# Relative-bias tables of a two-block decoder on Trainium2: skewed DMA reads in place of reversing matmuls, and another place for the small products

## What is computed

```python
def swiglu(x, w_gate, w_up, w_down):
    return (jax.nn.silu(x @ w_gate) * (x @ w_up)) @ w_down

def head_bias(table, dist):
    return jnp.moveaxis(table[rel_bucket(dist)].astype(jnp.float32), -1, 0)

# diff_attention, one block of 128 queries
dist = qpos[:, None] - kpos[None, :]
s = jnp.einsum('bqhcd,bkhcd->bchqk', qi, k, preferred_element_type=jnp.float32) * scale
s = s + head_bias(bias_table, dist)[None, None]
```

## Time and profile before

| | |
|---|---|
| median of 3 runs | 3522.79 us (3521.4 to 3523.41) |
| profiled execution, its own time | 3524.35 us |
| its span in the trace | 3522.6 us |
| PE busy | 3349.7 us, 95% |
| DVE / ACT / POOL busy | 1847.8 / 1566.2 / 143.4 us |
| mean DMA rate | 164 GB/s |
| chain that ended last | PE 88%, DVE 6%, ACT 4% |

### The profile page before, as it was taken

The page is one execution under the profiler, slowest core; times in us unless marked ns, Lnnn a source line. Parts: engine busy times, 40 slices in busy tenths (PEclk is TensorE's granted clock), DMA queues, the critical chain, the costliest instruction groups (busy, mean ns, idle before and its releaser), DMA issues.

```text
span 3522.6 us, 39807 instructions
## 1 busy us (share of the span) xinstructions
PE 3349.7 (95%) x16471; PEld 2785.5 (79%) x16471; DVE 1847.8 (52%) x2387; ACT 1566.2 (44%) x1918; POOL 143.4 (4%) x253
## 2 busy tenths in 40 slices
PE   8999999949999999999999999989999999999998
PEld 6898888737888888878888788977788788867886
DVE  5456454565455555455464554643554645534645
ACT  4344444424444444344344344455543544555444
POOL 0000000012000000000000000022000000121000
PEclk9999999969999999999899999989999999999999
DMA  6545555413555545555455545642455556523553
GB/s 209 191 156 179 191 180 191 157 60 112 190 180 191 168 144 191 179 184 187 143 178 183 177 156 190 169 126 96 135 192 173 173 187 179 144 97 119 188 188 111
DMA packets 323904, 576.24 MB, mean 164 GB/s; under 512 B 45257, under 2 KB 130352, under 8 KB 323596
## 3 DMA queue, kind: packets, MB, share of 16 engines
q1 hardware_dynamic: 321196, 566.71, 49.6%
q0 software_dynamic: 2384, 6.63, 0.7%
q10 hardware_dynamic: 144, 0.35, 0.0%
HBM read 571.53 MB, written 1.08 MB: 163 GB/s over the span
## 4 chain that ended last, share of the span: by engine, by line
PE 88%; DVE 6%; ACT 4%; issue 1%; DMA 0%; DVEq 0%; SPq 0%; ACTq 0%
PE up L1663 20%; PE up L1664 19%; PE up L1665 19%; PE acc L1663 8%; PE acc L1665 8%; PE acc L1664 8%; DVE w_lo L939 2%; ACT w_hi L559 2%; PE up L1938 1%; PE acc L1833 1%; PE up L2154 1%; DVE xT_lo L1051 1%; PE acc L1760 1%; ACT xT_hi L624 0%; PE acc L1840 0%
## 5 line engine op out<-in xcount | busy, mean ns | idle before, releaser
L939 DVE TENSOR_TENSOR w_lo<-raw,w_hi 128x2048 fp32r<-128x2048 f32 x543 | 1244.3, 2292 | 1349.2 <-ACT w_hi L559 1346.5
L559 ACT ACTIVATE w_hi<-raw 128x2048 fp32r<-128x2048 f32 x543 | 1040.7, 1917 | 1467.5 <-PE up L1665 1091.0
L1663 PE MATMUL up<-w_hi,xT_hi 128*128 128x512 f32 (+1 forms) x2500 | 993.5, 397 | 66.3 <-DVE xT_lo L1051 26.8
L1664 PE MATMUL up<-w_lo,xT_hi 128*128 128x512 f32 (+1 forms) x2500 | 982.5, 393 | 0.0
L1665 PE MATMUL up<-w_hi,xT_lo 128*128 128x512 f32 (+1 forms) x2500 | 981.8, 393 | 0.0
L1663 PEld LDWEIGHTS up<-w_hi,xT_hi 128*128 128x128 f32 x2500 | 476.1, 190 | 179.5 <-issue 47.0
L1665 PEld LDWEIGHTS up<-w_hi,xT_lo 128*128 128x128 f32 x2500 | 476.1, 190 | 99.4
L1664 PEld LDWEIGHTS up<-w_lo,xT_hi 128*128 128x128 f32 x2500 | 476.5, 191 | 94.6
L1663 PE MATMUL acc<-w_hi,ff_hi 128*128 128x512 f32 x1216 | 480.3, 395 | 3.5 <-DVE ff_lo L1070 3.5
L1665 PE MATMUL acc<-w_hi,ff_lo 128*128 128x512 f32 x1216 | 474.0, 390 | 0.0
L1664 PE MATMUL acc<-w_lo,ff_hi 128*128 128x512 f32 x1216 | 473.4, 389 | 0.0
(11 more groups left out here) (282 smaller groups left out, 2360.2 us busy)
## 6 DMA issues: line engine op xcount, KB each, us to landing
raw<-in_ffn_down SPq DMA_DIRECT2D x88, 1024.0 KB, 4.8
raw<-in_ffn_gate SPq DMA_DIRECT2D x80, 1024.0 KB, 5.1
raw<-in_ffn_up SPq DMA_DIRECT2D x80, 1024.0 KB, 5.1
raw<-in_ffn_wi SPq DMA_DIRECT2D x80, 1024.0 KB, 5.2
raw<-in_ffn_wo SPq DMA_DIRECT2D x44, 1024.0 KB, 4.8
raw<-in_w_in SPq DMA_DIRECT2D x38, 1024.0 KB, 5.1
raw<-in_conv_w_in SPq DMA_DIRECT2D x24, 1024.0 KB, 5.2
raw<-in_w_branch SPq DMA_DIRECT2D x12, 1024.0 KB, 5.0
```

The source lines that it names most:

```text
L559: nc.scalar.activation(w_hi[n % RING][:], raw[n % RING][:], ACT.Copy).then_inc(hi_ready, 1)
L939: nc.vector.tensor_tensor(w_lo[n % RING][:], raw[n % RING][:], w_hi[n % RING][:].bitcast(F32), ALU.subtract).then_inc(lo_ready, 1)
L1663: pe.matmul(ps, lh, rh, start=start, stop=False)
L1664: pe.matmul(ps, lh, rl, start=False, stop=False)
```

## The change

The tables stages move behind norms 8, 9 and 11, each directly in front of a feed-forward, and `after` and the two tests of `turned_x` look past them. The small products of part 1 are written into the banks up[2] and up[3], ahead of `first_pair`, which uses up[0] and up[1]; the feed-forward then waits for DVE's copies (`tab_dve`) before its second pair of banks. DVE scales the rows while it copies them. POOL stores every row 128 times, 383 elements each (20 x 128 rows) and a longer row of 511 for eight heads (8 x 128), and reads them with a skew of 382 (510) elements per partition straight into T and TCW. DVE picks TC out of TCW in part 2, which waits for both reads. The 30 products of 128x8, U, and the 10 reversing products with their copies are gone. The convolution's work area moves to another place in the arena.

```diff
--- before.py
+++ after.py
@@ -101,11 +101,9 @@
         plan += [("conv", i // 3)] if i % 3 == 0 else [("mla",)] if i == 1 else [("sg",)]
         plan += [("norm", 3 * i + 2), ("ffn", 1, i, 1)]
 
-    at = plan.index(("norm", 9))
-    plan[at:at] = [("tables", 0)]
-    at = plan.index(("norm", 10))
-    plan[at:at] = [("tables", 1)]
-    plan += [("tables", 2)]
+    for part, row in enumerate((8, 9, 11)):
+        at = plan.index(("norm", row)) + 1
+        plan[at:at] = [("tables", part)]
     for i in range(2):
         plan += [("norm", 12 + 4 * i), ("ffn", 2, i, 0), ("norm", 13 + 4 * i), ("mix", i)]
         plan += [("norm", 14 + 4 * i), ("ffn", 2, i, 1), ("norm", 15 + 4 * i), ("ple", i)]
@@ -188,8 +186,8 @@
 
         T = carve(0, 20, 256)
         TC = carve(5120, 8, 2 * NCMP)
-        U = carve(5376, 20, 256)
-        rv = carve(10496, 2, 384)
+        TCW = carve(5376, 8, 384)
+        rv_a, rv_c = arena[0:12, 10496:11008], arena[0:8, 13204:13588]
         lp = carve(11264, 2, 4, 64)
         prows = arena[0:64, 11776:11904]
         relb = arena[0:33, 11904:11924]
@@ -323,7 +321,8 @@
         fin_in = sem("fin_in")
         w2_in = sem("w2_in")
         fin_ready = sem("fin_ready")
-        scratch = nc.dram_tensor("bias_rows", (20, 384), F32, kind="Internal").ap()
+        scratch = nc.dram_tensor("bias_rows", (20, P, 383), F32, kind="Internal").ap()
+        scratch_cmp = nc.dram_tensor("cmp_rows", (8, P, 511), F32, kind="Internal").ap()
         vn_ready = sem("vn_ready")
         stored = sem("stored")
 
@@ -496,7 +495,7 @@
 
         def after(i):
 
-            return next((s for s in plan[i + 1:] if s[0] != "norm"), ("end",))
+            return next((s for s in plan[i + 1:] if s[0] not in ("norm", "tables")), ("end",))
 
         block = ctx.enter_context(nc.Block())
 
@@ -775,12 +774,9 @@
                 owed.append(n0 + 11)
 
             def tables(part):
-                arrive()
-                arrive()
-                settle()
                 if part != 1:
                     return
-                act.wait_ge(tab_dve, seen.next(tab_dve))
+                act.wait_ge(tab_dve, seen.next(tab_dve, 2))
                 nc.scalar.activation(ssh[:, 4:8], ssh[:, 0:4], ACT.Exp).then_inc(tab_act, 1)
 
             def mix(s, n0):
@@ -1366,15 +1362,27 @@
 
             def tables(part):
 
-                residual()
-                settle()
                 if part == 0:
+                    nc.vector.memset(rv_a[:, 384:512], NEG / HSCALE)
                     nc.vector.memset(relb, NEG).then_inc(arena_free, 1)
                     return
                 if part == 2:
-                    flipped_tables()
+                    dve.wait_ge(u_in, seen.next(u_in, 32))
+                    for t in range(NT):
+                        at = 159 - P * t
+                        last = nc.vector.tensor_copy(TC[:, :, NCMP * t:NCMP * t + NCMP],
+                                                     TCW[:, :, at:at + 16 * (NCMP - 1) + 1:16])
+                    dve.wait_ge(tab_act, seen.next(tab_act))
+                    for i in range(2):
+                        step(nc.vector.tensor_tensor(neglam[:, i:i + 1], ssh[:, 5 + 2 * i:6 + 2 * i],
+                                                     ssh[:, 4 + 2 * i:5 + 2 * i], ALU.subtract))
+                        step(nc.vector.tensor_scalar(neglam[:, i:i + 1], neglam[:, i:i + 1], -LAM_INIT[i], None, ALU.add))
                     return
                 dve.wait_ge(tables_in, seen.next(tables_in, 16 * 8))
+                dve.wait_ge(tab_pe, seen.next(tab_pe))
+                nc.vector.tensor_scalar(rv_a[:, 0:384], up[2][0:12, 0:384], 1.0 / HSCALE, None, ALU.mult)
+                nc.vector.tensor_scalar(rv_c, up[3][0:8, 0:384], 1.0 / HSCALE, None, ALU.mult).then_inc(rv_ready, 1)
+                nc.vector.tensor_copy(pos2[:].rearrange("p i v j -> p (i v j)"), up[2][:, 384:448]).then_inc(tab_dve, 1)
                 for i in range(2):
                     for j in range(2):
                         last = nc.vector.tensor_tensor_reduce(nwt[:], lp[:, i, 2 * j, :], lp[:, i, 2 * j + 1, :], 1.0, 0.0,
...
-                dve.wait_ge(tab_dve, seen.next(tab_dve))
-
-                dve.wait_ge(tab_pe, seen.next(tab_pe))
-                nc.vector.tensor_copy(rv[0:12, 0, :], acc[0][0:12, 0:384])
-                nc.vector.tensor_copy(rv[0:8, 1, :], acc[1][0:8, 0:384]).then_inc(rv_ready, 1)
...
-            def flipped_tables():
-                for g in range(10):
...
@@ -1945,6 +1930,8 @@
                 drain_banks()
                 gates, ups_ = [up[0][:], up[1][:]], [up[2][:], up[3][:]]
                 first_pair(n, FW, gates)
+                if held:
+                    pe.wait_ge(tab_dve, seen.next(tab_dve))
                 n += 2
                 for c in range(NFC):
                     if c > 1:
@@ -1982,38 +1969,14 @@
                 residuals[0] -= 1
 
             def tables(part):
-                if part == 0:
+                if part != 1:
                     return
-                if part == 2:
-                    flipped_tables()
-                    return
+                drain_banks()
                 pe.wait_ge(tables_in, seen.next(tables_in, 16 * 8))
-                pe.wait_ge(tab_dve, seen.next(tab_dve))
-                pe.matmul(acc[0][0:12, 0:384], relb[:, 0:12], one_hots[:, 0:384], start=True, stop=True)
-                pe.matmul(acc[1][0:8, 0:384], relb[:, 12:20], one_hots[:, 384:768], start=True,
-                          stop=True)
-                pe.transpose(acc[2][:, 0:64], prows, ident[0:64, 0:64])
-                for t in range(NT):
-                    for b in range(NCMP):
-
-                        at = C_OHF - C_KEPT + 256 + P * t - 16 * b - 31
-                        i = NCMP * t + b
-                        last = pe.matmul(acc[3][:, 8 * i:8 * i + 8], one_hots[:, at:at + P], relb[:, 4:12], start=True,
-                                         stop=True)
-                last.then_inc(tab_pe, 1)
-                pe.wait_ge(tab_dve, seen.next(tab_dve))
-
-            def flipped_tables():
-
-                pe.wait_ge(u_in, seen.next(u_in, 16))
-                pe.wait_ge(x_ready, QUARTERS * (1 + residuals[0]))
-                for g in range(10):
-                    if g >= 4:
-                        pe.wait_ge(tab_dve, seen.next(tab_dve))
-                    pe.matmul(acc[g % 4][:], consts[:, C_FLIP:C_FLIP + P],
-                              U[:, 2 * g:2 * g + 2, :].rearrange("p h j -> p (h j)"), start=True,
-                              stop=True).then_inc(tab_pe, 1)
-                pe.wait_ge(tab_dve, seen.next(tab_dve, 4))
+                pe.wait_ge(arena_free, 1)
+                pe.matmul(up[2][0:12, 0:384], relb[:, 0:12], one_hots[:, 0:384], start=True, stop=True)
+                pe.matmul(up[3][0:8, 0:384], relb[:, 12:20], one_hots[:, 384:768], start=True, stop=True)
+                pe.transpose(up[2][:, 384:448], prows, ident[0:64, 0:64]).then_inc(tab_pe, 1)
 
             def mix(s, n0):
 
@@ -2298,7 +2261,7 @@
                     mix(s, n0)
                 elif s[0] == "ple":
                     ple(s, n0)
-                if s[0] not in ("norm", "final"):
+                if s[0] not in ("norm", "tables", "final"):
                     turned_x = s[0] == "mix"
                 residuals[0] += s[0] not in ("norm", "tables", "final")
 
@@ -2362,12 +2325,19 @@
                                        A["nsa_cmp_pos_2"][i, v].rearrange("(j q) d -> j (q d)", q=2)
                                        ).then_inc(tables_in, 16)
                 pool.wait_ge(rv_ready, 1)
-                pool.dma_start(scratch[0:12, :], rv[0:12, 0, :]).then_inc(rv_stored, 16)
-                pool.dma_start(scratch[12:20, :], rv[0:8, 1, :]).then_inc(rv_stored, 16)
-                pool.wait_ge(rv_stored, 32)
-
-                askew = bass.AP(scratch.tensor, 0, [[1, P], [384, 20], [1, 256]])
-                pool.dma_start(U, askew).then_inc(u_in, 16)
+                def copies(row, n):
+
+                    return row.rearrange("h (o n) -> h o n", o=1).broadcast_to([n, P, row.shape[1]])
+
+                pool.dma_start(scratch[0:12], copies(rv_a[:, 0:383], 12)).then_inc(rv_stored, 16)
+                pool.dma_start(scratch[12:20], copies(rv_c[:, 0:383], 8)).then_inc(rv_stored, 16)
+                pool.dma_start(scratch_cmp, copies(rv_a[4:12, 0:511], 8)).then_inc(rv_stored, 16)
+                pool.wait_ge(rv_stored, 48)
+
+                askew = bass.AP(scratch.tensor, P - 1, [[382, P], [383 * P, 20], [1, 256]])
+                pool.dma_start(T, askew).then_inc(u_in, 16)
+                askew_cmp = bass.AP(scratch_cmp.tensor, P - 1, [[510, P], [511 * P, 8], [1, 384]])
+                pool.dma_start(TCW, askew_cmp).then_inc(u_in, 16)
 
             def mix(s):
 

...
```

More of the change, by code:

```diff
@@ L163, in build @@
         g_rows = arena[0:G_ROWS, 0:D]
-        zconv = carve(0, 2, TOK + 2)
-        yconv = carve(520, 2, TOK)
```

(6 more changed lines are left out.)

14 lines of the change are left out of this document (removed).

## The result

The changed kernel takes **3555.4 us** (median of 4 runs, 3553.86 to 3558.12) against 3522.1 us of the kernel before beside it (4 runs, 3521.03 to 3523.41). The ratio is 1.0096, 95% interval 1.0081 to 1.0111: slower by 33 us, where 46 us less was forecast. The profiled run took 3554.6 us, its span is 3552.8 us.

What follows compares the result with a forecast made beforehand. PE was taken to bound the kernel (busy 95%, 88% of the chain), so only shortening its queue counted. Removed 48.2 us less added 2.0 gave -46.2 from 3522.79, so 3476.6 us; range 3474 to 3494.

Steps and rivals of the forecast that it cites:

- Removed work, norms 9, 10 and 12: Boundaries at these norms, priced against sisters without a tables stage: gains of 7.7, 22.5 and 18.0 us, together 48.2 us.
- the further 1.7 us from the clock: Norm 10: a possible extra gain of 1.7 us on the diagonal products if the clock holds.
- Small work in front of the feed-forward: Behind norm 9: small products and PE's waits for `tab_dve` and the fourth tile add 2.0 us, bounds 1.2 and 5.
- Rival 1: Feed-forward behind norm 9: small work makes the fifth tile slip too, one period of 5.4 us lost, 3481; chance 0.06.
- Part 2 and the reads: Behind norm 11: small copies cost nothing (1 us without cover); reads fit, 58 us of transfers in about 290 us.
- rival 3: Part 2: skewed reads not back, DVE and all low parts wait; about 3725 us with a single engine; chance 0.04.
- The transfers: Behind norm 9: 10.2 MB beside the weights, a tile landing in about 10 us, cost nothing.
- the 11.9: Weight stream: a tile may land as late as 11.9 us after its issue at no cost.
- Rival 2: Feed-forward behind norm 9: slow stores from few partitions crowd the weights, 14 us lost, 3491; chance 0.24.
- quarter of the old read's: Assumed rate of the stores, against the old skewed read's 236 GB/s, making them last 102 us.
- a landing of 16 us: Assumed landing time of a weight tile beside the slow stores, each then 1.4 us late, 15 tiles long.
- Its formula for what a late landing costs: Each tile late by (landing - 11.9) / 3 us, times the tiles, less DVE's lead over PE of 6.5 us.

Runs made afterwards that it cites:

- x6: Changed kernel with its transfers cut into 29 pieces, each let go by the progress of the low parts, rows still on neighbouring partitions: 3475.41 us, ratio 0.9862.
- x1: Changed kernel with every row stored once in place of 128 times, reads the same size without skew, tables wrong: 3489.17 us, ratio 0.9901.
- x7: Changed kernel with rows stored once, no skew, tables wrong, and the two reads held back for three more tiles: 3480.51 us, ratio 0.9876.
- x10: Changed kernel with its three whole stores run one after another, not cut: 3546.47 us, ratio 1.006.
- x2: Changed kernel with the stored rows on every fourth partition in place of neighbours, same bytes and rows: 3492.51 us, ratio 0.9914.
- x4: Changed kernel with rows stored once into DRAM and the 128 copies made from there, DRAM to DRAM: 3500.41 us, ratio 0.9931.

## Why the prediction was wrong

- **Removed work, norms 9, 10 and 12: right.** Norm 10 gave 46.50 - 23.96 = 22.5 us (22.5 forecast; the further 1.7 us from the clock did not come), norm 12 gave 40.98 - 23.00 = 18.0 (18.0). For norm 9 the proof is x6, which keeps the change's every part but the pieces and the timing of its transfers: 190.05 us between the marks against 189.4, and 3475.4 us in all against 3476.6 forecast.
- **Small work in front of the feed-forward: right, a little low.** From 1490.68 to the second pair of tiles at 1518.73 are 28.05 us, where norm 3 has 25.7; that is 2.3, and 0.23 at the fourth tile. 2.6 us for 2.0. The parts were less well sized than the sum: PE waited 0.99 us for `tab_dve`, where 0.2 was forecast, and 0.23 us for the fourth tile, where 0.6 was. Rival 1 did not come: nothing slipped by a period.
- **Part 2 and the reads: right.** No wait for the reads in front of the attention; rival 3, the one on the losing side, did not happen.
- **The transfers: this step failed.** "Shared half and half, a tile lands in about 10 us, below 11.9: nothing." It took bytes per second as what two queues divide. They divide turns, one packet each, and a store packet from neighbouring partitions held an engine for 0.53 us. The tiles behind norm 9 landed in 40 to 86 us and not in 10, and the cost was 77.6 us and not 0. Ahead of the first turn came over 11 us without any weight packet, which no term of the sum had. One error more lay in the 11.9: it is a slack of the middle of a stage, and at its start there was less (x1 against x7: 9.03 and 2.35 us of waiting for the same reads).
- **Rival 2 had the mechanism and not its size.** It named the stores' 12 and 8 partitions, the turns, the tiles late, and 102 us of stores (106 measured). That 102 came so near was luck, as far as its own working goes: no row stands behind the "quarter of the old read's" rate. It then put in a landing of 16 us, again with no row behind it. Its own numbers gave more: 6.0 MB at 3.7 KB a packet are 1620 packets, over 102 us of 16 engines 102 x 16 / 1620 = 1.0 us each, and 32 turns behind 1.0 us are over 32 us for one tile (0.53 us and 20 us as measured), with three tiles in the ring, not a landing of 16. Its formula for what a late landing costs holds: with the measured median (59.2 - 11.9) / 3 = 15.8 us a tile, and for the 5.0 tiles that came 79 us, less the lead of 6.5 is 73, beside 71.5 of idle time. The upper end of the range, 3494, stood on the 16.

The chance of 0.04 for slower was an error of the same kind: the losing side was given only to the reads, and of rival 2, which by the text's own count stops being faster at 39 us, no price above 14 us was worked out. With the failed step put right the sum is 3476.6 + 0.6 (small work) + 77.6 = 3554.8, measured 3555.4. Since the 77.6 is itself read from that trace, this says only that nothing else in the kernel moved.

## What to carry to other kernels

A bulk transfer that runs beside a stream of weights is priced by packets: how long one of its packets holds an engine, how many stand in front of a tile's own on each engine, and so how many tiles come while it lasts; free GB/s price nothing (in x10 19 to 36% of the engines' time was idle while tiles waited). Cut it into pieces whose packets on one engine are few beside a tile's, and keep one piece open at a time or let the consumer's progress release them: here either turned 1.0096 into 0.986. A transfer that goes whole is better held back until the stage's first tiles are in (x7 against x1, about 9 us), and drawn from partitions that are spread out (x2, 63 us).

## What was not expected of the hardware

- Only moving the source rows from neighbouring partitions to every fourth brought the three stores from 106 to 41 us, at the same bytes and rows.
- Running whole stores one after another took 118 us in place of 107, and on the engines that a store used weights still passed only one packet for one; the shares 66.4, 43.9 and 45.7% show 12 and 8 of the 16.
- A tile issued behind an open backlog got no packet through for over 11 us in the changed kernel and for 5 us in x1, and only then one for one.
- Copies from DRAM to DRAM (x4) were no way out: 49 us for 6.0 MB, and 17 us of PE idle.
